# The shared expert's products as four matmuls of 32 weight columns

## What is computed

```python
def swiglu(x, w_gate, w_up, w_down):
    return (jax.nn.silu(x @ w_gate) * (x @ w_up)) @ w_down

# in moe_ffn: xf is 1024 x 1024, w_sg and w_su 1024 x 256, w_sd 256 x 1024
return routed + swiglu(xf, w_sg, w_su, w_sd)
```

## Time and profile before

| what | value |
|---|---|
| median of 3 runs | 1668.12 us (1663.58 to 1668.8) |
| the profiled execution: its own time | 1667.79 us |
| the profiled execution: span of the trace | 1666.0 us |
| mean granted TensorE clock over the span | 0.945 |
| shared jobs, 593.07 to 690.41 us | 97.34 us |
| routed jobs, 690.41 to about 1630 us | about 940 us |

### The profile page before, as it was taken

The page is one execution under the profiler, slowest core; times in us unless marked ns, Lnnn a source line. Parts: engine busy times, 40 slices in busy tenths (PEclk is TensorE's granted clock), DMA queues, the critical chain, the costliest instruction groups (busy, mean ns, idle before and its releaser), DMA issues.

```text
span 1666.0 us, 24640 instructions
## 1 busy us (share of the span) xinstructions
PE 1544.2 (93%) x6767; PEld 704.6 (42%) x6768; DVE 678.1 (41%) x884; ACT 302.4 (18%) x573; POOL 684.0 (41%) x631
## 2 busy tenths in 40 slices
PE   7789899998997689999999999999999999999991
PEld 3455455555555445433333333333333333333330
DVE  1223442524425242434444444444444444444440
ACT  1223223232232100011111111111111111111110
POOL 2000212022021140045656566565666566565652
PEclk9799998898988789999999999999999999999995
DMA  9201101011116052388899988987889989888925
GB/s 353 77 26 45 38 19 57 13 44 41 28 45 252 26 152 88 124 296 297 270 317 287 348 266 281 314 245 234 263 275 340 348 274 327 274 271 265 301 31 114
DMA packets 72032, 319.36 MB, mean 192 GB/s; under 512 B 14935, under 2 KB 16472, under 8 KB 46532
## 3 DMA queue, kind: packets, MB, share of 16 engines
q1 hardware_dynamic: 41764, 237.52, 38.7%
q0 software_dynamic: 30240, 81.50, 20.3%
HBM read 280.11 MB, written 60.89 MB: 205 GB/s over the span
## 4 chain that ended last, share of the span: by engine, by line
PE 87%; DMA 4%; DVE 3%; issue 2%; POOL 1%; SPq 1%; ACT 1%; POOLq 0%; DVEq 0%; ACTq 0%
PE psP L628 50%; PE psW L628 27%; PE psT L765 5%; DMA area<-in_x_dram 1%; PE psW L795 1%; DMA u_dram<-zrow 1%; PE psW L674 1%; PE psT L634 1%; DMA out_dram<-area 1%; DVE area L1228 1%; DMA area<-xn_dram,gidx 1%; DVE area L1124 1%; ACT area L909 0%; SPq L352 0%; PE psT L705 0%
## 5 line engine op out<-in xcount | busy, mean ns | idle before, releaser
L628 PE MATMUL psP<-wts,area 128*64 (+2 forms) x1344 | 586.5, 592 | 14.4 <-DVE area L1124 11.8
L628 PE MATMUL psW<-wts,area 128*64 128x512 f32 (+2 forms) x1592 | 430.0, 596 | 4.9 <-DVE wts L1450 4.2
L628 PEld LDWEIGHTS psP<-wts,area 128*128 128x128 f32 (+1 forms) x1344 | 223.9, 171 | 326.9 <-issue 320.2
L628 PE MATMUL psP<-wts,bias 128*64 (+1 forms) x688 | 306.6, 598 | 1.3 <-DVE bias L1348 1.3
L628 PE MATMUL psP<-area 128*64 128x512 f32 x640 | 283.2, 595 | 0.0
L628 PE MATMUL psP<-area,bias 128*64 128x512 f32 x624 | 277.6, 598 | 0.0
L628 PEld LDWEIGHTS psW<-wts,area 128*64 128x64 f32 (+1 forms) x1592 | 150.8, 149 | 257.4 <-issue 256.4
L571 POOL COPY gidx<-area 128x1 int32 (+1 forms) x83 | 205.1, 2471 | 83.8 <-PE psT L765 58.1
L588 POOL DMA_INDIRECT out_dram<-area,sidx x79 | 119.3, 1510 | 261.6 <-ACT area L1049 160.8
L1442 DVE COPY area<-wts 128x4096 f32 x81 | 186.2, 2299 | 97.2 <-issue 88.1
L588 POOL DMA_INDIRECT x_dram<-area,sidx x79 | 167.7, 2123 | 24.4 <-issue 24.4
(11 more groups left out here) (206 smaller groups left out, 994.3 us busy)
## 6 DMA issues: line engine op xcount, KB each, us to landing
wts<-in_w_exp_gate_dram SPq DMA_DIRECT2D x64, 1024.0 KB
wts<-in_w_exp_up_dram SPq DMA_DIRECT2D x64, 1024.0 KB
wts<-in_w_exp_down_dram SPq DMA_DIRECT2D x64, 1024.0 KB
wts<-in_w_in_dram SPq DMA_DIRECT2D x4, 2048.0 KB, 17.6
area<-in_x_dram SPq DMA_DIRECT2D x8, 512.0 KB, 3.2
wts<-in_w_out_dram SPq DMA_DIRECT2D x1, 4096.0 KB, 18.3
area<-u_dram SPq DMA_DIRECT2D x16, 256.0 KB, 2.9
xn_dram<-area POOLq DMA_DIRECT2D x8, 512.0 KB, 3.0
```

The lines of the kernel that those rows point to most:

```text
L628: return nc.tensor.matmul(out_, lhsT, rhs, start=start, stop=stop)
```

## The change

In `gate_up` and in `down` each matmul with 128 weight columns becomes four with 32 weight columns each: columns c to c+31 of the weights, for c = 0, 32, 64, 96, written to PSUM partitions c to c+31. The moving operand is the same for all four. The order is four matmuls for one k (or one n and f), then the next k. The semaphore increment stays on the last matmul. The routed jobs are not changed.

```diff
     HB = P // 2
+    QB = P // 4
...
                 for k in ks:
-                    i = mm(psP[:, par, :].rearrange("p (m f) -> p m f", m=2), xT[par][:, k, :], w[:, :, k, :], k == 0,
-                           k == KT - 1)
+                    for c in range(0, P, QB):
+                        i = mm(psP[c:c + QB, par, :].rearrange("p (m f) -> p m f", m=2), xT[par][:, k, c:c + QB],
+                               w[:, :, k, :], k == 0, k == KT - 1)
...
                         o = 2 * GUW + f * D + n * 512
-                        i = mm(psW[:, 2 + n, :], hT[:, f, :], wts[:, o:o + 512], f == 0, f == FT - 1)
+                        for c in range(0, P, QB):
+                            i = mm(psW[c:c + QB, 2 + n, :], hT[:, f, c:c + QB], wts[:, o:o + 512], f == 0, f == FT - 1)
```

## The result

| | before | after |
|---|---|---|
| median of 18 runs each | 1666.97 us (1663.58 to 1669.02) | 1669.83 us (1666.58 to 1671.8) |
| ratio | | 1.0016 (95%: 1.0009 to 1.0024) |

The changed kernel is 2.7 us slower by the ratio (1667 x 0.0016; its interval is 1.5 to 4.0 us). Forecast were 1670.2 us and a cost of 2.25 us.

What follows compares the result with a forecast made beforehand. The prediction took TensorE's matmuls as the bound (busy 1544.2 of 1666.0 us). 1667.79 us plus 2.25 for crossings gave 1670.04, from the three-run median 1670.37; 1670.2 was taken, range 1664 to 1675, or 1678 with the lower end of unclean overlap.

Steps and rivals of the forecast that it cites:

- 184 passes become 736 in the time of 184: Gate, up and down of the shared jobs: 184 rewritten passes, 79.0 us of TensorE, become 736, nothing added; chance 0.81.
- two strips at a time: Rival at the 184 passes: only two strips run at once, every pass time doubles, + 79.0 us, 1749 us; chance 0.06.
- four in turn: Rival at the 184 passes: the four strips run one after another, 237 us added, 1907 us; chance 0.02.
- overlap with a loss at every pass: Rival: each group of four loses 0.03 us (start skew) or 0.11 us (late weights), 1676 to 1691 us; chance 0.08.
- Why they overlap: On TensorE each strip advances by itself and instructions behind a waiting one are reached; two strips were seen to overlap wholly.
- The price of a crossing, 0.15 us: Each change between full width and strips costs 0.15 us where TensorE doesn't wait anyway; same price taken for 32 columns.
- The count, 15 new crossings: Job 0 one, job 1 none, loop step 1 two, steps 2 to 7 twelve; 15 x 0.15 = 2.25 us.
- the term for jobs 0 and 1: One new crossing, out of job 0's gate and up into bf16 matmuls, 0.15 us; job 1 nothing new.
- The tail slides by the same amount: Behind the shared jobs nothing gives time back; store, wait for gathered rows and expert weight loads move with job 7's down.
- a wait of 3.9 us that goes: Rival behind the shared jobs: the gather lands earlier and the 3.9 us wait goes, 1666.3 us; chance 0.03.
- The sum: Whole kernel: profiled 1667.79 us + 2.25 = 1670.04; from the median of three runs, 1670.37; 1670.2 taken.

## Why the prediction was right

- *184 passes become 736 in the time of 184*: right. 24.3 pass times for a job's products. Of the rivals, two strips at a time (1749 us), four in turn (1907) and overlap with a loss at every pass (1676 to 1691) are all out: bunches of four start 0.43 us apart, so four strips do four times the passes in one pass time of 0.429 us. No run shows a loss at every pass, neither the 0.03 nor the 0.11 us of those sums: with two strips and with four the bunches start 0.429 us apart, as wide passes do. A pass of 32 columns is no shorter than one of 128: a strip that runs alone, in the order with eight k in a row, starts one every 0.429 us too.
- *Why they overlap*: half right. The forecast read from the earlier trace rows that strips advance by themselves and that instructions behind a waiting one are reached. True, but only to a depth that no row showed. The order of the change puts two passes of a strip in a row (24.3 pass times a job), and four in a row still overlap (24.5); with eight it is 44.8. With the loop over the strips outside the loop over k (in all jobs but job 1), 16 in a row, the same matmuls cost 108 us more than with four. The forecast named the need to look further ahead and had no measure of how far that goes. That the order of the change lies inside what overlaps was luck.
- *The price of a crossing, 0.15 us*: right in kind, a little too high. 0.13 into strips of 32, 0.15 out of them into transposes, 0.28 for a pair against the 0.30 taken from strips of 64. The rows give a possible reason for the smaller price in: the loads take 0.110 us with 32 columns and 0.137 with 64 (the 0.14 that the forecast quotes from the earlier trace rows is a load of the transposes, with 128 columns). That the load is the cause is argued, not shown, and so is the reason that the forecast gave for the price as a whole, the loads that no longer run ahead. The one price was also too simple: before a wide float32 product it is 0.20, a crossing that the change itself doesn't have.
- *The count, 15 new crossings*: the loop steps fit, 0.28 in step 1 (614.15 to 620.25, 6.10 us, against 5.82), 6 x 0.285 = 1.71 in steps 2 to 7, and 0.13 at the end, before the first routed job, which the forecast had put at nothing and which wasn't followed up. Mis-sized was the term for jobs 0 and 1. It was put at + 0.15 and measured - 0.37 (21.32 us against 21.69). The crossing out of job 0 is there, 0.10 (the three bf16 matmuls take 0.19 us, before 0.09). But the four pieces of gate and up 1, counted as crossings that don't change, became about 0.06 us cheaper each (the first takes 1.92 us in the chain of waits, in that of the kernel before 1.98), and the way to the transposes of h was shorter by another 0.1 or so. The rest lies in gate and up 0, which starts at half the full clock (0.51 was granted up to 597 us in before) and takes 9.01, 8.92 and 9.20 us in the three profiles of before, 8.87 in both of after; whether the change has a part in that isn't shown.
- *The tail slides by the same amount*: this could not be seen, as the tail's own scatter (2.9 us up to the transposes behind the wait, 4.8 with the clock behind it) is larger than the whole effect. The forecast's rival, a wait of 3.9 us that goes, is part of that scatter: the unchanged kernel waits 1.1 us in one profile. The one profile by itself (span 1665.5 against 1666.0) would have said that the change is free.
- *The sum*: 2.25 forecast, 1.75 in the stage, 2.7 (1.5 to 4.0) timed. The 1 us between stage and timing is inside the interval and was not followed up. That the forecast lies between the two is partly chance: in the stage its errors, the term for jobs 0 and 1 above all, add up to 0.5 us too much.

## What to carry to other kernels

Splitting the columns of a float32 matmul (512 moving columns) into two or four strips over the same moving data cost no pass times on TensorE here as long as the order went round the strips at least every four passes (two float32 matmuls): a job's products took 24.3 pass times in four strips (10.43 us) and 24.4 in two (10.45 us) with two passes of a strip in a row, and 24.5 in four strips with four, where wide matmuls take 24 (10.30 us). With eight in a row it was 44.8. It was no gain either (ratio 1.0016): the reason to do it is strips that need different data, as in the routed jobs. What it does cost is each change between strips and full width, 0.13 to 0.20 us. So group what runs in strips, and don't put the loop over strips outside a long accumulation. Effects of 2 us in a kernel whose waits and clock scatter by 3 to 5 are read from the stage, not from the span.

## What was not expected of the hardware

The forecast had not expected that it matters how many passes of one strip stand in a row. With two or four of them all four strips start together (within 0.02 and 0.04 us). With eight or 16 the next strip's first pass starts when the one before has four passes left (641.058 against 641.052 with 16 in a row, 630.907 against 630.900 with eight), and gate, up and down take 44.8 pass times with eight in a row and 60.5 with 16, where 24 were needed; two strips of 64 columns with 16 in a row take 36.5. A model with four passes handed out for each strip, in program order, comes within 0.8 of a pass time of all five orders. It is an estimate from these times; no record shows how the engine holds its passes. A wide float32 product behind strips starts 0.20 us late (3.63 against 3.43 for down), a transpose 0.15 (1.02 against 0.87 for the eight), strips behind wide work 0.13 (7.00 against 6.87 for gate and up).
